# A hybrid attention and expert block on one core: group 1 of the mixer spread over more tiles, the last group's scores kept on chip

## What is computed

```
h = modulate(rmsnorm(x)); proj = h @ w_in
y_sb = stick_breaking_attention(...)         # 8 heads, strictly causal
y_sw = sliding_window_attention(...)         # own chunk and the one before
merged = sigmoid(ga) * (y_sb @ sb_proj) + sigmoid(gb) * (y_sw @ sw_proj)
x = x + gate1 * (merged @ w_out)
h2 = modulate(rmsnorm(x))
q = h2 @ w_q;  sub_s = q . sub_keys          # per row 8 heads x 2 x 128 scores
top 16 of each 128, top 16 of the 16 x 16 sums -> 16 experts a head
act = gelu(h2 . expert_u[e]);  y = sum(softmax * act * expert_v[e])
x = rmsnorm(x + gate2 * y)
```

## The kernel before

| group | H | QK | SWP | SW | MG | OUT | PREP | last PREP step |
|---|---|---|---|---|---|---|---|---|
| 1 | 0 | 15.4 | 78.6 | 93.0 | 109.4 | 155.0 | 181.6 | 214.2 |
| 2 | 235.0 | 256.4 | 389.6 | 410.6 | 434.7 | 504.2 | 540.6 | 590.3 |

## Time and profile before

### The profile page before, as it was taken

One profiled execution on the slowest core, in us unless ns is written; L12 is line 12 of the kernel. 1 busy time (PEld: TensorE's weight loads), 2 busy tenths in 40 slices (PEclk: granted clock), 3 DMA queues, 4 the chain that ended last, 5 costly groups with the idle time before them and its releaser, 6 DMA issues.

```text
span 3479.6 us, 35550 instructions
## 1 busy us (share of the span) xinstructions
PE 2187.0 (63%) x11116; PEld 979.8 (28%) x11116; DVE 2024.9 (58%) x4779; ACT 1152.5 (33%) x3650; POOL 1121.8 (32%) x1033
## 2 busy tenths in 40 slices
PE   5878677668976856777667877774433443344333
PEld 2566533244433412232233432341100000000000
DVE  1021556665655465777586667556666666666644
ACT  2111335642222235666543223222322232223222
POOL 0000133323322232444333333333344344434442
PEclk9999888889987978988888988886665565665655
DMA  9433679988999898999999999999999999999998
GB/s 367 171 133 111 258 296 367 357 330 347 372 371 394 332 419 326 416 390 396 368 370 412 421 421 385 392 420 421 392 421 421 421 399 421 421 421 391 421 421 335
DMA packets 197214, 1274.27 MB, mean 366 GB/s; under 512 B 21192, under 2 KB 38632, under 8 KB 54048
## 3 DMA queue, kind: packets, MB, share of 16 engines
q0 software_dynamic: 147616, 1074.03, 75.7%
q1 hardware_dynamic: 49408, 197.96, 14.6%
HBM read 1247.51 MB, written 24.40 MB: 366 GB/s over the span
## 4 chain that ended last, share of the span: by engine, by line
PE 40%; DMA 35%; ACT 10%; issue 9%; DVE 5%; POOL 1%; SPq 0%; POOLq 0%; DVEq 0%; ACTq 0%
DMA arena<-in_uv,idx_r 26%; PE pb L969 13%; PE pb L752 5%; PE pb L684 5%; ACT dg L1206 3%; PE pb L714 3%; ACT L105 2%; PE pb L687 2%; PE pb L773 2%; DMA arena<-in_w_ada 2%; DMA arena<-in_w_q 2%; PE pb L955 2%; DVE arena L1524 2%; PE pb L848 1%; PE pb L659 1%
## 5 line engine op out<-in xcount | busy, mean ns | idle before, releaser
L606 POOL DMA_INDIRECT arena<-in_uv,idx_r x1024 | 1118.7, 1093 | 2329.7 <-PE pb L969 1719.5
L1524 DVE CUSTOM_DVE_ANT_0 arena<-arena 128x1024 f32<-128x1024 f32 x1024 | 1249.3, 1222 | 743.1 <-DMA arena<-in_uv,idx_r 703.6
L969 PE MATMUL pb<-arena,dg 128*32 128x512 f32 x4096 | 735.3, 855 | 866.6 <-ACT dg L1206 866.6
L969 PEld LDWEIGHTS pb<-arena,dg 128*32 128x32 f32 x4096 | 134.3, 138 | 1357.0 <-ACT dg L1206 1060.9
L1200 ACT ACTIVATE gl<-dots 128x4 f32<-128x4 f32 x256 | 52.4, 205 | 989.0 <-DVE dots L1524 987.9
L752 PE MATMUL pb<-arena 128*128 128x384 f32 (+1 forms) x768 | 250.7, 484 | 66.2 <-issue 51.8
L105 ACT ACT_TABLE_LOAD x177 | 227.1, 1283 | 133.1 <-DVE dots L1524 77.0
L684 PE MATMUL pb<-arena 128*128 128x384 f32 (+1 forms) x768 | 238.8, 465 | 15.9 <-DMA arena<-in_w_mg 15.2
L1206 ACT ACTIVATE dg<-ig,gl 128x32 f32<-128x32 f32 x1024 | 245.1, 310 | 8.4 <-ACT gl L1200 0.2
L1195 ACT ACTIVATE ig<-istack,gate_r 128x32 f32<-128x32 f32 x1024 | 241.6, 308 | 0.0
L752 PEld LDWEIGHTS pb<-arena 128*128 128x128 f32 x768 | 153.6, 205 | 158.6 <-issue 95.1
(11 more groups left out here) (156 smaller groups left out, 2232.4 us busy)
## 6 DMA issues: line engine op xcount, KB each, us to landing
arena<-in_w_mg SPq DMA_DIRECT2D x24, 1536.0 KB, 10.8
arena<-in_w_ada SPq DMA_DIRECT2D x12, 2048.0 KB, 17.3
arena<-in_w_q SPq DMA_DIRECT2D x24, 1024.0 KB, 12.7
arena<-in_uv,idx_r POOLq DMA_INDIRECT x1024, 12.0
arena<-in_w_qk SPq DMA_DIRECT2D x12, 1024.0 KB, 13.6
arena<-in_w_out SPq DMA_DIRECT2D x3, 4096.0 KB, 16.2
arena<-in_w_sw SPq DMA_DIRECT2D x3, 3072.0 KB, 11.6
arena<-in_x SPq DMA_DIRECT2D x16, 512.0 KB, 15.2
```

Source lines behind the costliest of these rows:

```text
L606: pool.indirect_dma_start(ring[:, i % RING, :], None, uv, bass.IndirectOffsetOnAxis(ap=idx_r[:, b % 2, 4 * n + c:4 * n + c + 1], axis=0)). ...
L969: m = pe.matmul(pb[32 * c:32 * c + 32, VACC + i, :], dg[:, STEP * n // 4 % 2, c, :], ring[:, (STEP * g + c - first) % RING, D + i * HALF:D ...
L1524: dve.tensor_tensor_reduce(u, h2rep[:, slot(b, c), :], u, 1.0, 0.0, ALU.mult, ALU.add, dots[:, i % 8:i % 8 + 1]).then_inc(dots_done, 1)
```

## The change

- `RATES` goes from (1.9, 2.9, 1.9) to (1.9, 2.5, 2.1), and a step of PREP now has a length in tiles, `SPREAD` = (4.7, 8.0, 9.0). Group 2 starts 2 tiles after the last PREP step of group 1.
- The due time of chunk n's selection moves from 32(n - 2) to 32n - 52, so 12 tiles later. SP's read of the scores is issued up to 10 tiles ahead of it (at the earliest 1.5 tiles ahead of the time at which the scores count as ready).
- For the last group (blocks 5 to 7) ACT copies the scores to `kept`, in the place that held `hT`, `ysb` and `ysw`. They are not written to memory and not read back, and DVE selects in place. DVE then waits for ACT's copy (`pr_se`) and not for a DMA (`in_tk`). ACT's wait for the write two heads before is gone there too.

```diff
-RATES = (1.9, 2.9, 1.9)
+RATES = (1.9, 2.5, 2.1)
+SPREAD = (4.7, 8.0, 9.0)
+LEAD = 52
...
-            self.now = begins[g]
+            self.now = begins[g] if g < len(begins) else self.now + 2
...
-                self.item("PREP", g, h, 18 * part)
-            self.now += 2
+                self.item("PREP", g, h, SPREAD[g] * RATES[g])
...
-        at = Plan([-probe("PREP", 0, 2) - 36, 0.0, 235.0])
+        at = Plan([-probe("PREP", 0, 2) - 36, 0.0])
...
+        kept = f(A0, GMAX * HEADS * 2 * NKEYS).rearrange("p (b h q n) -> p b h q n", b=GMAX, h=HEADS, q=2)
...
+        def ready_at(b, m):
+            return at("PREP", GROUP[b], 2 * m + 1, part(GROUP[b], 11) + 4)
+
         def topk_at(b, m):
             n = CHUNKS * b + m
-            ready = at("PREP", GROUP[b], 2 * m + 1, part(GROUP[b], 11) + 4)
-            return ready if n < 2 else max(32.0 * (n - 2), ready)
+            return ready_at(b, m) if n < 2 else max(32.0 * n - LEAD, ready_at(b, m))
...
                 def parked(g):
                     GB, T = SIZE[g], SIZE[g] * P
+                    if g + 1 == GROUPS:
+                        return
...
                 def keys():
-                    for b in range(NB):
+                    for b in range(FIRST[-2]):
...
-                            yield topk_at(b, m) - 1.5
+                            yield max(topk_at(b, m) - 10, ready_at(b, m) - 1.5)
...
                             act.wait_ge(pr_s, 2 * n + p + 1)
+                            if g + 1 == GROUPS:
+                                act.activation(kept[:, 0:GB, h, p, :], pb[:, BGB + 2 + p, 0:T].rearrange("p (b n) -> p b n", b=GB), ACT.Copy).then_inc(pr_se, 1)
+                                continue
...
+                        elif b < FIRST[-2]:
+                            dve.wait_ge(in_tk[n % 2], 16 * ((n + 1) // 2))
                         else:
-                            dve.wait_ge(in_tk[n % 2], 16 * ((n + 1) // 2))
+                            dve.wait_ge(pr_se, 2 * HEADS * (GROUPS - 1) + 4 * (m + 1))
...
-                                op = yield from top16(vals[q][:, h, :], kidx[q][:, h, :], tk[:, n % 2, 256 * h + 128 * q:256 * h + 128 * q + 128])
+                                place = tk[:, n % 2, 256 * h + 128 * q:256 * h + 128 * q + 128] if b < FIRST[-2] else kept[:, b - FIRST[-2], 2 * m + h, q, :]
+                                op = yield from top16(vals[q][:, h, :], kidx[q][:, h, :], place)
```

## The result

| | before | after |
|---|---|---|
| median of 4 runs | 3503.9 us (3499.89 to 3506.99) | 3410.36 us (3405.42 to 3419.26) |
| the profiled execution's own time | 3481.42 us | 3405.42 us |
| its span | 3479.6 us | 3403.6 us |
| moved by DMA | 1274.27 MB | 1267.97 MB |

The ratio is 0.9737, 95% interval 0.9712 to 0.9761, which is 92 us (the medians differ by 93.5). A fourth execution of the kernel before puts its median at 3503.9 us. The forecast was 3460 us with a range from 3418 to 3495, so the sign was right and the size less than half of what was measured. Between the two profiled executions the difference is 76 us, and that is what these rows can show.

A forecast was written before the change was run, and what follows sets the result against it. DMA was taken as the bound, with idle time beside group 1 to fill. Terms -45 - 17 + 8 + 8 + 6 = -40 us gave 3441 from the profiled 3481.4, 3461 from the median 3500.8; forecast 3460 us, range 3418 to 3495.

The forecast's parts named there:

- Four terms of the sum: Group 1 spread -45 us, group 2 denser +8, chunk 8 at the block's edge +8, x for group 2 +6.
- Keeping: Last group's scores: 8 writes and 12 reads, 6.3 MB, no longer moved; -17 us, ends -12 and -40.
- What bounds the kernel: DMA's queue of transfers carries the kernel; beside group 1 its share is 0.90, with 82 us of DMA time lost.
- Single waits of 16 to 17 us stay where they are: Group 1: ring places cover only some of these waits, so three quarters of 60 us were taken, -45 us.
- The stage sum: Group 1 from H to PREP: bytes with added tiles at 400 GB/s, never under the row's time; 60 us gained.
- reads ahead: Score reads issued 10 tiles ahead remove seven of eight VectorE waits (76.9 us in all); beside group 1 not counted again.
- Chunk 8 at tile 256: Publication moves to 4 tiles ahead of first use, DMA idles and selection steps hold dot products; +8 us, ends +3, +20.
- x for group 2: At group 2's start the read of x comes only 2 to 4 tiles ahead of use; +6 us, ends 0, +15.
- Group 2 denser: H to OUT of group 2 has 26.8 fewer tiles beside the same work; +8 us, ends 0 and +20.
- rival 3: DMA fills up entirely beside group 1 and group 2 costs nothing; -85 us, 3416 us, chance 0.18.
- Rival 1: Mixer stretches with the tiles, no room found, or lower clock in PREP; 3496 to 3506 us, chance 0.09.
- rival 2: Edge at tile 256 breaks, pipeline stops 70 to 90 us; slower, 3508 to 3530 us, chance 0.06.

The follow-up runs named there:

- The plan alone: Kernel before with only the new rates, PREP spread and group 2 starting two tiles behind group 1; ratio 0.985, 52 us faster.
- the change again: The whole change, unaltered, run once more as reference on another chip; ratio 0.9759 to the kernel before.
- first and fourth group: Two sets of follow-up kernels, each set on one chip against the kernel before, which had medians of 3500.8 and 3503.2 us there.
- keeping alone: Kernel before with only the last group's scores kept on chip; ratio 0.9958, 15 us faster.
- second and third group: Two sets of follow-up kernels, each set on one chip against the kernel before, which had medians of 3481.3 and 3486.8 us there.

## Why the prediction was too small

The runs split the missing 52 us in two. Four terms of the sum belong to the plan: -45 + 8 + 8 + 6 = -23. The plan alone measured -52. The later due time had no term and measured some -23. Keeping was right to 2 us.

- **What bounds the kernel** was right. DMA full is the bound, its idle time beside group 1 is the room, and the window shares moved up as described. The three marks set for group 1 came out: its end at 1306 us (1315 forecast), about 3.3 us a tile, and a DMA share of 0.95. This is group 1 in the trace of the change, and in the second profile of the same kernel (the change again):

```profile
437.10:1306.30 869.20, 654.00 (x3251) 309.06 (x3250) 534.89 (x1270) 330.21 (x1017) 295.58 (x267) 0.89 0.95 385
```

```profile
434.50:1297.00 862.50, 659.33 (x3250) 314.03 (x3250) 535.50 (x1270) 330.37 (x1017) 298.50 (x267) 0.89 0.95 388
```

- **The step that failed first** is "Single waits of 16 to 17 us stay where they are and ten ring places cover only some of them, so I take three quarters". The stage sum before that cut said 60 us. By the rows it was 53 in the change's trace. In the second profile the group takes 862.5 us where it took 824.9, so 98 - 38 = some 61. Stage by stage the growth was forecast as 3, 0, 3, 7, 4 and 18 us (pairs, SWP, SW, MG, OUT, PREP) and measured as 4, 10, -3, 8, 3 and 19 in the first of them. The single stages were off by up to 10 us and the sum came right. The cut had no row behind it, and 15 us of the miss are its size. The likely reason, which no run isolates, is that the single waits were in the stage's own time already, which the sum never went below, so taking a quarter off counted them twice.
- **The due time had no term at all**, and this is the largest single part of the miss. The prediction followed the reads ("reads ahead") and asked what waits for them. It never asked what else lies at tile 128k when a selection starts and another is published there. On the plan that one edit is worth 21 to 24 us in the first and fourth group. In the second it is 8 us alone and 8 to 16 within the change. It was priced at nothing, and no work was named that hides it.
- **The 19.4 us between the profiled execution and the median were carried along.** The forecast took 40 us off either number, as if the offset were a constant. It was not. The change's profiled execution is 5 us under its median. In the trace of before the windows of 12 tiles at the three late edges take 34 us with DMA at 0.91 to 0.93, as the one at tile 768 shows (these rows of before were not read for the forecast):

```profile
2793.70:2828.10 34.40, 20.05 (x176) 4.77 (x176) 19.00 (x45) 13.53 (x44) 10.70 (x11) 0.66 0.93 371
```

  In the parts run with the same due time on a chip where the kernel before has a median of 3500.8 they take 37 to 39 us at 0.82 to 0.88. The publication at that edge shows a difference. The first two rows are of the trace of before, the last two of keeping alone:

```profile
2803.49 0.46 PE L937 MATMUL pb<-picks,ident 128*32 128x16 f32 x32 [0.59 <-ACT arena L1184]
2804.23 0.23 ACT L1170 ACTIVATE idx_r<-pb 128x32 uint32<-128x32 f32 x1 [0.89 <-PE pb L937]
```

```profile
2801.40 0.46 PE L940 MATMUL pb<-picks,ident 128*32 128x16 f32 x32 [0.60 <-ACT arena L1190]
2804.98 0.23 ACT L1176 ACTIVATE idx_r<-pb 128x32 uint32<-128x32 f32 x1 [3.72 <-remote]
```

  ScalarE's copy of the expert numbers waits for the last of the 32 short matmuls. Their record is equally long in both, yet the copy starts 0.3 us behind it in the one and 3.1 us in the other ("remote" means that the profile names no instruction that ended the wait), and TensorE's next piece waits for the copy. All 18 traces divide this way: over the last 12 chunks the median is 0.2 us in the trace of before and in those of the second and third group, and 2.4 to 2.8 us in the trace of the change and in those of the first and fourth group. The kernel before has medians of 3481.3 and 3486.8 us on the chips with the prompt copy and 3500.8 and 3503.2 on those with the late one. So the trace that the forecast rested on was of a prompt execution, the timed runs had the longer medians, and the 76 us between the two traces compare unlike executions. The second profile of the change is a prompt one, and its last dot product comes 90 us ahead of that of before. The two sizes of the late edges (some 34, and 37 to 39 us) divide the traces with the old due time in the same way. By tile 512, where both kernels have done the same work, keeping alone is 7 us behind the trace of before, and at the three late edges it loses some 12 us more. Together that is the size of the 19.4 us. That the late copy is the whole cause was not shown. It fits that the later due time gave 8 to 16 us on the chip with 3481.3 and over 20 us on those with 3500.8 and 3503.2.
- **Keeping**: -17 forecast, 15 measured twice, alone and in the whole. Right, and the row that carried it was the right one. The 54 us of the estimate with a fixed part for each DMA did not come.
- **Reads ahead** were not counted beside group 1, and rightly: VectorE stood 60 us less and nothing was gained.
- **Chunk 8 at tile 256**: +8 forecast. The order and both durations came about as worked out (11.2 us for the 24 steps where 10 were said, 12.0 us of POOL's wait), the price was 2 us. What was missed is that six gathers leave together when the numbers come.
- **x for group 2**: +6 forecast. ScalarE's waits for it rose from 1.7 us to 9.2 us. DMA's share in H of group 2 is 0.95, so the loss is 1 to 2 us. Over-priced by some 4 us. These are the wait and the window, of the change:

```profile
ACT arena L999 <- DMA arena<-in_x: 9.2, 3, 4.0
```

```profile
1306.30:1332.70 26.40, 12.62 (x69) 4.07 (x69) 18.62 (x55) 12.09 (x41) 8.76 (x9) 0.63 0.95 374
```

- **Group 2 denser**: +8 forecast. The run with the old density was 11 us faster with overlapping intervals. What the plan alone leaves is smaller: 60 from the stages less 52 measured is 8 us for chunk 8, x and density together.
- **The range** ended at 3418, above the 3416 of its own rival 3. By the ends given for the terms the sum reaches down to -82 - 40 + 0 + 3 + 0 = -119, which is 3382. The 3435 of the prediction has no working.
- **Rivals.** Rival 3 (DMA fills up, 3416 us) was the nearest in its number, and for the wrong reason in part: over 20 of its us are the due time. Rival 1 and rival 2 did not happen, and the granted clock in PREP rose from 0.83 to 0.87 and not down. The lower clock weighed there cost nothing: TensorE's busy time did not thin out, since the added tiles' sums filled the stage (68% busy before, 154.2 of 217.9 us or 71% after). Where it did thin out, in the run with only PREP spread, TensorE is 56% busy and the granted clock is 0.78.

## What to carry to other kernels

Where the bound resource idles beside dense stages of an in-order program, sum over the stages the bytes at the full rate, never under the stage's own time. Here that sum gave 60 us where 53 and 61 were measured, and a discount on top of it, for waits that the stage's time holds already, spoilt it. An edit of a due time is an edit of everything that shares the moment, so list what each engine has to do at the old moment and at the new one. 60 us of waits on VectorE cost nothing here, and one of 12 us on POOL cost 2 us of DMA time, while a wait of 14 us with three of 5 us ahead of it emptied DMA. Before two traces are compared, look at one piece that is the same in both: if its length differs, the difference between the traces is not the edit's alone.

## What was not expected of the hardware

With the old due time the same kernel's block edges come in two sizes with the same instructions: 12 tiles in 32.5 to 34.4 us in the two traces with the prompt copy and in 37.4 to 39.1 us in the four with the late one. With the later due time they take 31 to 33 us everywhere. TensorE's granted clock there is 0.63 to 0.67 in both sizes (once 0.76), and 0.66 to 0.78 with the later due time. Why ScalarE's copy behind the 32 short matmuls starts 0.2 us behind their record in half of the traces and 2.4 to 2.8 us in the other half was not found. All traces from one chip agree in it.
